# Weight pieces of the mixer split behind the eviction of the unit that leaves their buffer

## The reference, cut to what matters

```
h    = layer_norm(x, ln0_g, ln0_b)
proj = h @ w_in                       # qkv, a, bt, z, xc, gb, gc, qm, gl
qkv  = silu(causal_depthwise_conv(qkv, conv_qkv))         # width 4
y_a  = gated_delta_rule(qkv, ...) * silu(z)
y_b  = gb * causal_depthwise_conv(gc * xc, conv_mix)      # width 3
y_m  = attention(qm, mem @ w_mem_kv)
merged = sum over b of sigmoid(gl[b]) * (y[b] @ w_br[b])
h    = layer_norm(ALPHA * h + merged @ w_o, ln1_g, ln1_b)
h    = layer_norm(ALPHA * h + moe_ffn(h, ...), ln2_g, ln2_b)
```

## Time and profile before

| | |
|---|---|
| median of three runs | 1283.3 us (1281.4 to 1283.37) |
| profiled execution | 1282.62 us, span of its trace 1280.9 us |
| TensorE (PE) busy | 1217.3 us, 95% |
| VectorE (DVE) busy | 392.6 us, 31% |
| ScalarE (ACT) busy | 241.3 us, 19% |
| GpSimd (POOL) busy | 146.1 us, 11% |
| DMA | 453.62 MB, mean 354 GB/s |
| mean granted clock of TensorE | 0.991 of full |

### The profile page before, as it was taken

One profiled execution on the slowest core, in us unless ns is written; L12 is line 12 of the kernel. 1 busy time (PEld: TensorE's weight loads), 2 busy tenths in 40 slices (PEclk: granted clock), 3 DMA queues, 4 the chain that ended last, 5 costly groups with the idle time before them and its releaser, 6 DMA issues.

```text
span 1280.9 us, 16880 instructions
## 1 busy us (share of the span) xinstructions
PE 1217.3 (95%) x7135; PEld 616.2 (48%) x7135; DVE 392.6 (31%) x784; ACT 241.3 (19%) x387; POOL 146.1 (11%) x106
## 2 busy tenths in 40 slices
PE   6989999999999999999999999999999999999996
PEld 5789999998843333333333333333333333333332
DVE  5375553434521221221221221221112222122224
ACT  4355345444310000000000000000000000000001
POOL 8223432455200000000000000000000000000000
PEclk9899999999999999999999999999999999999998
DMA  9533323475799999999999999999999999999994
GB/s 299 200 133 132 115 85 128 171 304 196 277 401 420 398 427 426 420 431 428 430 435 428 431 430 427 433 431 427 430 430 430 432 432 426 429 432 430 426 425 179
DMA packets 49512, 453.62 MB, mean 354 GB/s; under 512 B 6110, under 2 KB 10283, under 8 KB 31019
## 3 DMA queue, kind: packets, MB, share of 16 engines
q1 hardware_dynamic: 49450, 452.71, 85.2%
HBM read 451.64 MB, written 1.05 MB: 353 GB/s over the span
## 4 chain that ended last, share of the span: by engine, by line
PE 72%; DMA 19%; DVE 3%; ACT 2%; POOL 2%; issue 1%; SPq 0%; ACTq 0%; DVEq 0%; POOLq 0%
PE bank L1386 27%; DMA late<-in_w_gate_up_dram 19%; PE bank L1459 13%; PE bank L1203 6%; PE bank L1204 5%; PE bank L1205 5%; PE bank L1472 4%; PE bank L1357 3%; PE bank L1372 2%; PE bank L1447 1%; ACT late L1175 1%; POOL w_lo L758 1%; ACT w_hi L1079 1%; PE bank L1467 1%; PE bank L559 1%
## 5 line engine op out<-in xcount | busy, mean ns | idle before, releaser
L1386 PE MATMUL bank<-late 128*64 128x512 f32 x1632 | 368.1, 598 | 10.4 <-DMA late<-in_w_gate_up_dram 10.2
L1386 PEld LDWEIGHTS bank<-late 128*64 128x64 f32 x1632 | 112.6, 137 | 242.2 <-issue 217.6
L1459 PE MATMUL bank<-late 128*64 128x512 f32 x816 | 182.5, 599 | 5.3 <-ACT late L1175 5.3
L1203 PE MATMUL bank<-act_hi,w_hi 128*128 128x256 f32 x448 | 130.1, 290 | 6.9 <-POOL w_lo L758 3.7
L1204 PE MATMUL bank<-act_lo,w_hi 128*128 128x256 f32 x448 | 126.5, 282 | 0.0
L1205 PE MATMUL bank<-act_hi,w_lo 128*128 128x256 f32 x448 | 126.4, 282 | 0.0
L1802 DVE TENSOR_SCALAR late<-bank 128x512 f32<-128x512 f32 x32 | 22.1, 692 | 306.2 <-PE bank L1386 306.1
L1459 PEld LDWEIGHTS bank<-late 128*64 128x64 f32 x816 | 56.9, 138 | 112.8 <-issue 104.4
L1386 PE MATMUL bank<-raw,late 128*64 128x512 f32 x416 | 93.4, 596 | 3.2 <-DMA raw<-in_w_gate_up_dram 3.2
L758 POOL TENSOR_TENSOR w_lo<-raw,w_hi 128x1024 fp32r<-128x1024 f32 x33 | 82.0, 2487 | 117.0 <-ACT w_hi L1079 116.9
L1203 PEld LDWEIGHTS bank<-act_hi,w_hi 128*128 128x128 f32 x448 | 85.1, 190 | 9.3 <-issue 4.1
(11 more groups left out here) (320 smaller groups left out, 1247.6 us busy)
## 6 DMA issues: line engine op xcount, KB each, us to landing
late<-in_w_gate_up_dram SPq DMA_DIRECT2D x38, 4096.0 KB, 31.8
late<-in_w_down_dram SPq DMA_DIRECT2D x51, 2048.0 KB, 30.6
late<-in_w_gate_up_dram SPq DMA_DIRECT2D x26, 2048.0 KB, 13.5
raw<-in_w_gate_up_dram SPq DMA_DIRECT2D x10, 4096.0 KB, 31.7
raw<-in_w_down_dram SPq DMA_DIRECT2D x13, 2048.0 KB, 32.9
raw<-in_w_in_dram SPq DMA_DIRECT2D x8, 2048.0 KB, 7.8
early<-in_w_in_dram SPq DMA_DIRECT2D x6, 2048.0 KB, 7.6
raw<-in_w_gate_up_dram SPq DMA_DIRECT2D x6, 2048.0 KB, 10.6
```

Source lines behind the costliest of these rows:

```text
L1203: mm(o, l_hi, r_hi, start=start, stop=False)
L1386: ins = mm(bk[64 * c:64 * c + 64, :], x_slotT[:, k % 4, 64 * (k // 4):64 * (k // 4) + 64], w[:, kk, at + 512 * c:at + 512 * (c + 1)], star ...
L1459: ins = mm(ps[3][64 * c:64 * c + 64, :], hidT[:, kk, 64 * q:64 * q + 64], w[:, kk, c * 512:(c + 1) * 512], start=(q == 0 and kk == 0), sto ...
```

## The change

In `mixer_schedule`, for every unit that uses one piece, `("prep", q+3)` is put behind the unit and no longer ahead of it. Entries that use four pieces (`vm`, `wo`) keep their order, and entries of the delta rule stay behind both. So ScalarE does its part of the unit (eviction, or `silu`) first and hi(q+3) then; VectorE does its eviction first and lo(q+3) then, where lo is its own. TensorE's order, SyncE's order and the transfers are the same, and GpSimd's list keeps its order too, since it has no part of these units.

```diff
@@ -153,9 +153,12 @@
             n = 4 * (s[-1] == 0)
         if n:
             uses[s] = list(range(q, q + n))
-            out += [("prep", m + SPLITS) for m in uses[s] if m + SPLITS < 4 * N_MIX]
+            pieces = [("prep", m + SPLITS) for m in uses[s] if m + SPLITS < 4 * N_MIX]
             q += n
-        out.append(s)
+
+            out += pieces + [s] if n > 1 else [s] + pieces
+        else:
+            out.append(s)
     assert q == 4 * N_MIX
     return out, uses
```

## The result

The changed kernel takes 1287.19 us, the median of five runs (1285.41 to 1289.35), beside 1283.15 us for the kernel before. The ratio is 1.0041, 95% interval 1.0028 to 1.0054: 4.0 us slower by the medians, 5.3 by the ratio. Measured again later it gave 1285.54 beside 1281.39 us, ratio 1.0040 (1.0026 to 1.0055). The profiled execution took 1287.15 us, its span is 1285.4, which is 4.5 more than before. Lines behind the edit have moved by three (1079 is now 1082, 1058 is 1061, 758 is 761).

A forecast was written before the change was run, and what follows sets the result against it. Bound by the mixer's TensorE until 337 us, then the experts' weight stream. Loss 4.0 + 1.5 or 5.1 + 1.0, less 3.1, gives +2.4 or +3.0; +2.8 taken on the median 1283.3 gives 1286.1 us, range 1282.0 to 1289.0.

The forecast's parts named there:

- the loss: At `z 2`, piece 22 comes late because its cast stands behind `silu 11`: 3.97 or 5.11 us lost.
- First place: `qkv 4` to `qkv 8`: `qkv 4` starts 1.30 us sooner, lost again at `qkv 6` waiting for piece 14; sum 0.0.
- Second place: `z 1`: its bank is free early but piece 21 is late; start 99.80 instead of 99.99, gain 0.19 us.
- Third place: `z 2`: piece 22 late behind `silu 11` and VectorE's squares; start 106.80 or 107.94, loss 3.97 or 5.11 us.
- The other bound: At `z 2`, lo(23) follows VectorE's squares and keeps GpSimd out; start 107.94, loss 5.11 us.
- The clock: TensorE at half clock behind the stall at `z 2`: 1.5 us behind the shorter stall, 1.0 behind the longer; bounds 0 and 1.5.
- rival 2: The clock falls at `qkv 6` too, behind 3.8 us idle: adds 1.5 us, 1287.6; chance 0.18.
- Later gains: Shorter TensorE waits at `lx3`, the `score` units, `gate 0 0` and `br 0 7`: 3.1 us, bounds 1.5 and 3.5.
- Rival 1: Gains cover the loss at `z 2`: GpSimd isn't shut out or the clock doesn't fall; 1283.0 to 1285.3, chance 0.22.
- Rival 3: A table load ahead of the cast costs 1.28 us more at each of two places: 1288.7; chance 0.02.
- Rivals 4: Faster: `silu 11` isn't late and only the gains are left, 1280.2; chance 0.05.
- 5: The stream of weights hides the mixer's shift, so the end doesn't move: 1283.3; chance 0.03.

The follow-up runs named there:

- experiment 3: The changed kernel, but piece 22 is prepared ahead of `qkv 11` as before: 1281.3 us, ratio 0.9991 to the kernel before.
- 1: The changed kernel, but at all `qkv` units the pieces stay ahead of the unit: 1277.61 us, ratio 0.9966 to the kernel before.
- experiment 6: The changed kernel with unread filler matmuls: 32 ahead of `z 2` 1288.55 us; 16 there 1281.89 us; with 16 more ahead of `qkv 6` 1281.99 us.
- experiments 4: The changed kernel, but piece 14 is prepared ahead of `qkv 3` as before: 1284.67 us, ratio 1.0008 to the kernel before.
- 8: The changed kernel, but ScalarE's own list keeps casts first at `qkv` units: 1274.96 us, ratio 0.9936; with 8 filler matmuls ahead of `qkv 6` 1275.41 us.

## Why the prediction came out right

**The direction and the place.** The forecast was 1286.1 us; 1287.19 was measured. In the profiled execution +2.8 us was forecast and +4.5 measured, so the number is off by more in the trace than in the medians. What was on record as "the loss" is the loss: without the one entry of piece 22 the wait at `z 2` and its slow clock are gone (experiment 3, where 2.4 of the 8.1 us to `lx0` remain, by then made at `qkv 6`), and without all `qkv` entries nothing but gain is left (1).

**First place.** The forecast had `qkv 6` at 74.56 instead of 74.00; it is 74.88, of which 0.19 is there at `qkv 0` already. Its idle time is 3.92 us for the 3.8 forecast. Right.

**Second place.** The wait of `z 1` turned from one for the bank to one for the piece, 1.20 us where 1.3 stood. The start is not 0.19 sooner but 1.7 us later, all of it from `qkv 6`: its own lateness and the fallen clock behind it.

**Third place.** From `z 1` to `z 2` the forecast had 106.80 - 99.80 = 7.00 us, with GpSimd let in behind the squares; measured 108.65 - 101.72 = 6.93. The other bound, with VectorE's lo(23) getting in first, is not what happened: lo(23) itself was held to 3.36 us. Right to 0.1 us. But the wait here, 3.85 us, isn't the longest of the mixer, as was forecast; that at `qkv 6` is, with 3.92.

**The clock is the term that was mis-sized.** The forecast took 1.5 us, behind `z 2` alone. Measured: the fall at `qkv 6`, rival 2, did come (1.5 us by experiment 6, as that rival had it), and the one at `z 2` costs 2.3 us by the same experiment, in this trace, since the clock stayed down for nearly the whole of 107 to 114 us, about twice the stretch of the earlier trace rows. The nearest row was a single stretch behind a single stall, and I took its length for a bound where it was one sample. It wasn't a certain one either: at the place of that row the second trace of the changed kernel has a stall of 2.85 us with 1.00 granted from 29 to 36 us. So what happened is rival 2 on top of the forecast, with a dearer fall.

**Later gains.** Forecast 3.1 us, measured 3.7. From `br 1` on 1.7 us for 1.5; ahead of it 2.0 for 1.7. The eviction for `score 1` did come behind the exps of `score 0`, as was said, but TensorE's own step ended just as late, and the whole half microsecond was won.

**Terms together.** 3.97 at `z 2`, + 1.5 and + 2.3 for the two falls, - 3.7, make +4.1; 0.2 from the later start of the trace and about as much from `qkv 6` complete the 4.5 of the spans.

**What was luck.** The forecast itself had no fallen clock at `qkv 6`. Rival 2 had it, with a chance of 0.18; it came, and its 1287.6 is nearer to the 1287.19 than the 1286.1 of the forecast. The clock was taken 2.3 us too low (1.5 for 3.8), and the gains, 0.6 too low, made up for a part of it. The direction doesn't hang on that: by the stretches the loss of 8.1 us is more than twice the gain of 3.7.

**The rivals.** Rival 1 didn't occur, since the clock did fall, but its balance is near what experiment 6 shows: with the clock held at both places the median is level with before, 1281.99 beside 1282.64 us. From `qkv 0` to `br 0 7` that trace is still 1.5 us longer than before, 1.1 of it from the slow clock in its early part. Rival 3, a load ahead of the cast that costs more than behind it, didn't occur: 1.28 us, then 0.01 to the activation, in both orders. By the drain of the Trainium skill, "ScalarE: Activation LUTs", section "What ACT_TABLE_LOAD costs", the cast of piece 14 would have come 1.4 us later than it did; the trace doesn't agree. Rivals 4 and 5 didn't occur: the stretch to the end is the same and the mixer's loss came through.

## What to carry to other kernels

"Eviction first, split afterwards" holds for an engine whose part of the unit waits only for the unit. Where that part waits for another engine (`silu` for VectorE's eviction) or brings a table load, what is put behind it inherits that wait, so the order has to be chosen for each engine and not in one list: between `qkv 0` and `br 0 7` the same idea in two lists won 4.4 us where the single list lost 4.4 (8.0 won and 4.0 lost by the medians). Look for the one entry in hundreds where a wait is special, and where the granted clock can fall behind a stall of TensorE, as it did here behind those of 2.2 us and more at `qkv 6` and `z 2`, allow for more than the stall's length.

## What was not expected of the hardware

- The clock fell behind a stall of 2.2 us (experiments 4 and 8) and held behind 1.9 us at the same place and at 315 us behind 2.15 us. But the length of a stall alone doesn't decide it. In the trace of before it was at half behind 1.79 us at 48.78 (granted 0.58 from 48 to 52 us), with another stall of 1.23 us just ahead, at 46.32; and in the second trace of the changed kernel it held behind 2.85 us at 31.72 (1.00 from 29 to 36 us), where the earlier trace rows has 0.76 behind 2.71. It stayed down for nearly 7 us behind one of 3.85 us in one trace, and a second trace of the same kernel had the long fall behind `qkv 6` instead (0.50 granted from 72 to 78 us), so the place of the long one changes between executions. The same kernel lost 8.1 us to `lx0` in both traces.
- VectorE and GpSimd pass the two-input operations to and fro in turn: squares, lo(22), lo(23), lo(24), each of the held ones 1.0 to 2.1 us longer than alone.
- A matmul of 128 float32 columns, as the filler uses it, is two instructions and 0.23 us; 32 of them are 7.3 us.
